# A hybrid diffusion layer on one core: the second half of a modulation placed inside another tile's products, wider loads, and two chunks loaded earlier

## The reference, cut to what matters

```
m = silu(c) @ w_ada + b_ada            # 6 vectors of 1024: shift, scale, gate, twice
h = rmsnorm(x) * g * (1 + scale) + shift
u = h @ w_in                           # 1024 -> 2*512 (convolution) + 384 + 256 + 64
conv: a * sigmoid(g) -> depthwise conv, 31 taps -> LayerNorm -> silu
attention: low-rank q, kv, a rotary key; 4 heads
x = x + gate * rmsnorm([conv, attention] @ w_out)
h = modulated rmsnorm(x); router over 4 groups of 8 experts; top 2 experts of each token
x = x + gate * rmsnorm(sum over chosen experts of gated MLP)
```

## Time and profile before

| | us |
|---|---|
| median of 3 runs | 716.09 (715.47 to 720.83) |
| profiled execution, its own time | 715.66 |
| its span | 713.7 |
| PE busy in the span | 592.5 (83%) |
| DVE busy in the span | 259.1 (36%) |
| ACT busy in the span | 148.9 (21%) |

### The profile page before, as it was taken

One profiled execution on the slowest core, in us unless ns is written; L12 is line 12 of the kernel. 1 busy time (PEld: TensorE's weight loads), 2 busy tenths in 40 slices (PEclk: granted clock), 3 DMA queues, 4 the chain that ended last, 5 costly groups with the idle time before them and its releaser, 6 DMA issues.

```text
span 713.7 us, 9157 instructions
## 1 busy us (share of the span) xinstructions
PE 592.5 (83%) x3662; PEld 346.3 (49%) x3662; DVE 259.1 (36%) x445; ACT 148.9 (21%) x299; POOL 85.9 (12%) x103
## 2 busy tenths in 40 slices
PE   0889799999999999989999658889989977777800
PEld 0656556655555455544445555455545544444300
DVE  2315799999444054411322470111011100000133
ACT  3320000012225254431222401110110110000142
POOL 6000000600000000000211016121112111110011
PEclk9999999999999999999999959999999999999955
DMA  9999936000005460008121981999999999999378
GB/s 338 354 368 342 380 125 236 14 0 1 0 1 222 170 264 1 0 25 328 60 118 59 372 322 26 341 367 422 423 424 423 423 424 425 424 425 390 141 299 163
DMA packets 49281, 172.00 MB, mean 241 GB/s; under 512 B 5722, under 2 KB 14267, under 8 KB 36938
## 3 DMA queue, kind: packets, MB, share of 16 engines
q1 hardware_dynamic: 41216, 156.11, 55.1%
q0 software_dynamic: 6736, 13.59, 6.2%
q10 hardware_dynamic: 1274, 1.52, 0.6%
HBM read 161.48 MB, written 17.06 MB: 250 GB/s over the span
## 4 chain that ended last, share of the span: by engine, by line
PE 60%; DMA 17%; SPq 10%; DVE 5%; ACT 3%; issue 3%; PEld 1%; DVEq 0%; ACTq 0%; POOLq 0%; POOL 0%; PEldq 0%
PE ps L1284 14%; DMA arena<-in_w_down 10%; PE ps L1468 10%; SPq L435 9%; PE ps L1533 8%; PE ps L1443 5%; PE ps L1549 5%; PE ps L1289 4%; PE ps L1285 4%; DMA arena<-in_w_ada 3%; PE ps L1452 3%; PE ps L1302 2%; PE ps L1368 2%; DMA x<-in_x_sample 1%; PE ps L1422 1%
## 5 line engine op out<-in xcount | busy, mean ns | idle before, releaser
L1284 PE MATMUL ps<-arena 128*128 128x512 f32 x256 | 132.1, 598 | 1.1 <-issue 1.1
L1533 PE MATMUL ps<-arena 128*64 128x256 f32 x992 | 111.4, 380 | 13.5 <-DMA arena<-in_w_up 6.4
L1533 PEld LDWEIGHTS ps<-arena 128*64 128x64 f32 x992 | 72.1, 137 | 55.9 <-issue 13.2
L1011 DVE SCALAR_TENSOR_TENSOR arena<-arena 128x655 f32<-128x655 f32 x116 | 95.0, 897 | 0.4 <-issue 0.2
L1549 PE MATMUL ps<-arena 128*64 128x512 f32 x256 | 63.4, 640 | 20.5 <-DMA arena<-in_w_down 10.6
L1285 PEld LDWEIGHTS ps<-arena 128*128 128x128 f32 x256 | 48.8, 191 | 61.5 <-issue 61.5
L1289 PE MATMUL ps<-cst,arena 128*128 128x128 f32 (+2 forms) x349 | 53.0, 294 | 25.4 <-DVE arena L950 16.8
L1468 PE MATMUL ps<-arena 128*128 128x512 f32 x160 | 69.2, 593 | 0.9 <-ACT arena L833 0.9
L1289 PEld LDWEIGHTS ps<-cst,arena 128*128 128x128 f32 (+2 forms) x349 | 44.1, 179 | 36.8 <-issue 32.4
L1285 PE MATMUL ps<-arena 128*128 128x128 f32 (+1 forms) x256 | 50.9, 280 | 0.0
L1250 DVE COPY arena<-ps 128x1024 f32<-128x1024 f32 x15 | 18.4, 1224 | 87.3 <-PE ps L1549 87.3
(11 more groups left out here) (246 smaller groups left out, 547.3 us busy)
## 6 DMA issues: line engine op xcount, KB each, us to landing
arena<-in_w_up SPq DMA_DIRECT2D x15, 2048.0 KB, 30.9
arena<-in_w_down SPq DMA_DIRECT2D x15, 2048.0 KB, 32.3
arena<-in_w_gate SPq DMA_DIRECT2D x14, 2048.0 KB, 29.6
arena<-in_w_ada SPq DMA_DIRECT2D x12, 2048.0 KB, 14.2
arena<-y_d SPq DMA_DIRECT2D x10, 512.0 KB, 7.0
arena<-in_w_in SPq DMA_DIRECT2D x8, 512.0 KB, 12.6
arena<-in_w_out SPq DMA_DIRECT2D x1, 4096.0 KB, 12.7
arena<-ada_d SPq DMA_DIRECT2D x8, 512.0 KB, 6.1
```

Of the source, the lines that this page charges most:

```text
L1011: ins = dve.scalar_tensor_tensor(dst, src, w, dst, ALU.mult, ALU.add)
L1284: mm(pp(name)[:, 0:TS], lhs(k), rhs_s(k), start=k == 0, stop=k == steps - 1)
L1533: last = mm(ps[a:a + ROWS, s, n * FE:(n + 1) * FE], src[:, k, a:a + ROWS], w[:, j, k * FE:(k + 1) * FE], start=k == 0, stop=k == KD - 1)
```

## The change

- The first half of `g1` moves ahead of the second half of `g0` and `a0`, right behind `ada(1)`; `modt1` stands between its blocks k = 1 and k = 2. The second half of `g1` follows `ada(2)`.
- `modt1` and `ada2` get PSUM slot 2 by name (`BESIDE`) and take no turn in the rotation; the groups behind keep their order of slots, two slots on.
- The columns of tiles 2 and 3 are loaded as two transfers with runs of 256 floats, in place of four with runs of 128, and counted on `wc_in[2]`.
- Chunks 6 and 7 are issued behind `wQ` and ahead of `w_uq` and `w_ukv`.
- The products that keep PE busy during routing write to the bank that goes with the shifted slots.

```diff
+BESIDE = {"modt1": 2, "ada2": 2}
...
-        names += [f"g{m}", f"a{m}"] + (["ada1", "modt1"] if m == 0 else []) + [f"ada{m + 2}"]
+        names += (["g0", "a0", "ada1", "g1", "modt1", "ada2"], ["a1", "ada3"], ["g2", "a2", "ada4"], ["g3", "a3", "ada5"])[m]
...
-    place = {name: (n % 4, n // 4) for n, name in enumerate(order)}
+    turns = [name for name in order if name not in BESIDE]
+    homes = [BESIDE[name] if name in BESIDE else turns.index(name) % 4 for name in order]
+    place = {name: (homes[n], homes[:n].count(homes[n])) for n, name in enumerate(order)}
...
-            def conv_weights(m):
+            def conv_weights(m, width=P):
                 for a in (C + m * P, m * P):
-                    sp.dma_start(wC[:, :, a:a + P], w_in_v[:, :, a:a + P]).then_inc(wc_in[m], 16)
+                    sp.dma_start(wC[:, :, a:a + width], w_in_v[:, :, a:a + width]).then_inc(wc_in[m], 16)
...
-            for m in range(2, CM):
-                conv_weights(m)
+            conv_weights(2, 2 * P)
             sp.wait_ge(ada_used, 4)
             sp.dma_start(wQ, w_in_v[:, :, 2 * C:]).then_inc(wq_in, 16)
+            for n in range(6, 8):
+                ada_chunk(n)
             sp.dma_start(wuq, i["w_uq"][0].rearrange("(k p) n -> p k n", p=P)).then_inc(wuq_in, 16)
             sp.dma_start(wukv, i["w_ukv"][0].rearrange("(k p) n -> p k n", p=P)).then_inc(wukv_in, 16)
-            for n in range(6, NCH):
+            for n in range(8, NCH):
                 ada_chunk(n)
...
-            def modulation(n):
-
-                ada(n)
+            def turn_modulation(n):
+
                 name = f"modt{n}"
...
                 for k in range(4 * n, 4 * n + 4):
+                    if name == "g1" and k == 2:
+                        turn_modulation(1)
...
             pe.wait_ge(wc_in[0], 32)
-            for n in range(2):
-                if n == 1:
-                    modulation(1)
-                half_project("g0", C, n)
-                half_project("a0", 0, n)
+            half_project("g0", C, 0)
+            half_project("a0", 0, 0)
+            ada(1)
+            pe.wait_ge(wc_in[1], 32)
+            half_project("g1", C + P, 0)
+            half_project("g0", C, 1)
+            half_project("a0", 0, 1)
             ada(2)
-            for m in range(1, CM):
-                pe.wait_ge(wc_in[m], 32)
+            half_project("g1", C + P, 1)
+            project("a1", lambda k: wC[:, k, P:2 * P])
+            ada(3)
+            pe.wait_ge(wc_in[2], 32)
+            for m in range(2, CM):
...
-                    mm(ps[:, 1, 0:P], ones[:], ident, start=True, stop=True)
+                    mm(ps[:, 2 * place[f"rl{NT - 1}"][0] + 1, 0:P], ones[:], ident, start=True, stop=True)
```

More of the change, by code:

```diff
@@ L1326, in modulation @@
                 done(last, name)
-            modulation(0)
+            ada(0)
+            turn_modulation(0)
             begin(pe, "vt")
```

## The result

| | before | after |
|---|---|---|
| median, us | 716.86 | 707.96 |
| lowest to highest of the usual runs, us | 713.93 to 720.83 | 705.88 to 711.58 |
| profiled execution, own time, us | 715.66 | 710.73 |
| its span, us | 713.7 | 708.8 |

(8 runs of each; one run of the kernel before took 3488.77 us. It is left out of the range but counts in the median of 716.86; without it the median is 716.09.) The time after over the time before is 0.9905, with a 95% interval of 0.9875 to 0.9934: 6.8 us faster, between 4.7 and 9.0. The medians differ by 8.9, or by 8.1 without that one run, the two profiled executions by 4.9. The predicted 9.15 us is on the high side of what was measured, and the question is where up to half of it went in the profiled execution.

The account below looks back on a forecast made before the run. PE's own work bounds the kernel up to the experts, then expert weights that PE's progress releases. Front losses of 9.64 us less a 0.29 gap and 0.2 for chunk 7 give 9.15 us: median 706.9, range 704.5 to 712.5.

Parts of the forecast that it names:

- The losses of the front and their removal: PE from `ada(1)` to `ada(4)`: losses of 9.64 us go, less a 0.29 gap; `ada(4)` at 96.90, not 106.25.
- The modulation hides: At `modt1`, two blocks of `g1` cover DVE's rows and two more ACT's scale and shift, removing 2.55 us idle.
- Tile 1's columns: `g1` needs them at 44.81; they should land at 42.3, 2.5 us ahead.
- Chunks 6 and 7 in time: Earlier queue place saves 5.6 us, wider runs 2.2; chunk 7 lands at 77.2, just meeting `ada(3)`'s need near 77.4.
- the widening: Longer runs for tiles 2 and 3's columns save 2.2 us of landing time; rival that it brings nothing, 0.14.
- The 0.2 us charged for PE's wait: In `ada(3)`, chunk 7 was taken to just meet the need, so 0.2 us came off the 9.35 gain.
- the base of the sum: Stretch from `ada(1)` to `ada(4)` in the first profile: 9.35 us to gain, leaving 52.38 us from `ada(1)`'s end.
- The rest follows: Behind the front DVE is some 3.4 us earlier, level with the rotary key's product at 178.0; ACT's lateness stays hidden.
- that rival: Expert weights stream at their own pace from a fixed start and swallow the gain; time stays 716; chance 0.05.
- The late clock ahead of the experts: Rival: the clock rises later, slowing the first pair's gate and up products by 0 to 4.2 us; chance 0.10.

Follow-up runs that it names:

- four profiles: Changed kernel profiled three times, plus once with extra products keeping PE busy in the routing; ratios to the kernel before 0.9905, 0.988, 0.9899 and 0.9867.
- three profiles of before: Kernel before profiled twice unchanged and once with extra products in the routing; front from `ada(1)` to `ada(4)` 65.43, 65.89 and 61.90 us.
- the other two: Repeats of the unmodified changed kernel against the kernel before, on other chips: ratios 0.988 (0.9854 to 0.9905) and 0.9899 (0.9863 to 0.9935).
- its second profile: Kernel before run again unchanged, against itself: ratio 1.0006 (0.9972 to 1.0039); first gate and up products 8.61 us.
- those eight others: Profiles without added routing products, two with PE's old order and six with the new; first gate and up products took 8.47 to 8.76 us.
- the changed kernel's third: Changed kernel run once more without modification, against the kernel before: ratio 0.9899 (0.9863 to 0.9935).
- the one with the early chunks: Changed kernel with chunks 6 and 7 issued ahead of `wQ` too; ratio to the kernel before 0.9916 (0.9891 to 0.9941).
- its three variants: Against the kernel before: only PE's new order and slots, 0.9996; only the new loads, 0.9908; changed kernel with 128-float runs for tiles 2 and 3, 0.9924.

## Why the prediction held, and which term was too large

The direction, the mechanism and the range held: 707.96 for 706.9, in 704.5 to 712.5. Point by point:

- *The losses of the front and their removal.* Right in each place: no gap at the modulation, the upper clock behind it, `ada(3)` whole, `ada(4)` within 0.1 us of the forecast.
- *The modulation hides.* Right. The transposes started at 47.23 without idle time, predicted 47.00, and no block waited for its scale and shift. Tile 1's columns were never waited for.
- *Chunks 6 and 7 in time.* The mechanism was right and its two parts measured, in pairs of single profiles: 5.4 us for the place in the queue, against 5.6, and 2.3 for the widening, against 2.2. The 0.2 us charged for PE's wait were 0, 0.83, 0 and 1.89 us in four profiles, a mean of 0.7.
- *The term that was too large* is the base of the sum, 9.35 us of losses taken from one execution. Chunk 7's lateness in the kernel before is itself variable: 3.04, 4.07 and 1.76 us of idle time. The front of before averages 64.4 us, not the 65.43 of that profile, which is 1.0 less to gain; and that of after 56.6, not the 56.3 which the sum implied. So 7.8 us, where the sum had 9.15, and the ratios and the 8.1 us between the medians agree with it. With three profiles of before that spread over 4 us this is the best reading and not a proof: 9.15 us would be a ratio of 0.987, which the interval of the first comparison excludes by a hair and the other two contain.
- *The rest follows.* DVE and POOL did not come in the way, though DVE's slack is now used up: it came to the rotary key's product without idle time, under a microsecond after PE had it.
- *The expert phase passed the gain on*, so that rival is out. The last weights land when PE lets them: from the start of the second pair's gate and up products to the landing of the last `w_down` it is 232.8 to 233.3 us in three profiles of before and 232.8 to 233.6 in five with the new order (the chip with the standstill described below left out). The last rows of both chains, first before, then after:

```profile
636.13 36.03 DMA arena<-in_w_down
...
672.30 5.37 PE ps L1549 x16
```

```profile
624.34 43.57 DMA arena<-in_w_down
...
668.04 5.37 PE ps L1564 x16
```

- *The late clock ahead of the experts*, given 0.10 as a cost of the change, is real in size (1.34 us in the products, 0.82 in the transposes), but the kernel before has it too, in its second profile; no run shows it as a cost of the change.

What stays open is why the gather took 4.55 us in the first profile of before and 5.6 to 6.1 in those eight others, and what decides in which executions the attention's last products meet a lower clock. The last products of the last pair are a third such place: they took 5.4 us in seven of the eight profiles with the new order and 3.7 in three of the four with the old one. That is 1.7 us at the very end, and whether the change has a part in it was not tested.

## What to carry to other kernels

Filling a gap on the engine is worth little or nothing if the next thing it needs is a transfer that is late already: the order alone gave 0.9996, the loads alone 0.9908. Look first at what stands ahead of that transfer in its queue and how long its runs are. And take a loss that hangs on a transfer's landing from several executions, since one profile's wait of 3 us was 1.8 to 4.1 in three. Where the profile shows TensorE's granted clock falling in an idle stretch ahead of a heavy phase, a few dozen products without use are worth a try: 49 more of them gave 0.9958 on the kernel before.

## What the runs showed of the hardware

- Loads from HBM with runs of 512 B moved 282 to 339 GB/s over the stretch from 50 to 60 us in five profiles, where runs of 1024 B moved 385 to 394 in five others; with the rest of the queue alike it was 313 against 385. The longer runs also came in half as many transfers, which no run tells apart. In the first profile of before it was 252 over the part with short runs alone.
- The granted clock fell to its lower level within the 7.57 us in which PE did nothing, and stayed at 0.50 through the products that PE had there before, with gaps between them, until the gather had been issued. In two profiles (the changed kernel's third, and the one with the early chunks) it was up again for the eight transposes, which took 1.18 and 1.16 us in place of 1.98, and fell back for the first of the gate and up products. With products through those 7.57 us it stayed at 1.00.
- On the first chip of the experiments, ACT stood still for 15 us in the first expert pair, in the changed kernel as in its three variants; the profile puts the wait down to a source outside the core's own engines ("remote"). PE idles 7.5 to 7.6 us behind it, the second pair starts 17.2 us after the first in place of 10.8 (second profile of before), and its gate and up products take 8.5 to 10.1 us in place of 7.15. That is some 8 to 9 us, near the 9.4 by which the kernel before is slower on that chip, but no profile of the kernel before was taken there. It was not seen on the other chips; what it is stays open.

```profile
ACT arena L894 <- remote: 15.3, 1, 15.3
```
